# A decoder layer in split fp32: the second cross query goes ahead of the memory product, one root for all query norms, GpSimd adds the cross heads

## What is computed

```python
h = rms_norm(x, attn_norm)
q, k, v, xq = split(h @ w_in, [1024, 1024, 1024, 256])
mix = stick_breaking(q, k, v)                       # 16 heads of 64
mk, mv = split(rms_norm(mem, mem_norm) @ w_mem_kv, [256, 256])
p = softmax(rms_norm(xq, xq_g) @ rms_norm(mk, xk_g).T * SCALE)   # 4 heads, 1024 x 256 each
x = x + concat(mix, p @ mv) @ w_out
x = x + swiglu(rms_norm(x, ffn_norm), w_gate, w_up, w_down)
```

## Time and profile before

| | us |
|---|---|
| median of 3 runs | 1426.36 (1424.12 to 1427.22) |
| the profiled execution | 1431.33, span 1429.5 |
| PE busy | 1377.2 (96% of the span) |
| DVE, ACT, POOL busy | 949.7, 655.3, 186.3 |

### The profile page before, as it was taken

The page is one execution under the profiler, slowest core; times in us unless marked ns, Lnnn a source line. Parts: engine busy times, 40 slices in busy tenths (PEclk is TensorE's granted clock), DMA queues, the critical chain, the costliest instruction groups (busy, mean ns, idle before and its releaser), DMA issues.

```text
span 1429.5 us, 20494 instructions
## 1 busy us (share of the span) xinstructions
PE 1377.2 (96%) x6988; PEld 1127.6 (79%) x6988; DVE 949.7 (66%) x1346; ACT 655.3 (46%) x1120; POOL 186.3 (13%) x155
## 2 busy tenths in 40 slices
PE   6999999899989999699999999999999999999999
PEld 5777788788878888577887788888888888888887
DVE  5567879687968888786347857455565645656455
ACT  7566566566666666573245413324232232422321
POOL 0000000000000000214014311112111120211200
PEclk9989999999999999899999999999999999999999
DMA  6100101001000101003300212111112111121103
GB/s 236 30 17 22 30 23 31 24 23 30 23 23 23 37 17 44 30 23 110 104 16 15 89 52 66 45 47 43 63 42 64 51 44 59 44 60 58 44 30 133
DMA packets 90136, 70.23 MB, mean 49 GB/s; under 512 B 3792, under 2 KB 75472, under 8 KB 90064
## 3 DMA queue, kind: packets, MB, share of 16 engines
q1 hardware_dynamic: 90064, 69.23, 15.6%
HBM read 65.03 MB, written 4.19 MB: 48 GB/s over the span
## 4 chain that ended last, share of the span: by engine, by line
PE 90%; ACT 4%; DVE 2%; issue 2%; POOL 1%; DMA 1%; SPq 0%; ACTq 0%; DVEq 0%; POOLq 0%
PE ps L1284 27%; PE ps L313 17%; PE ps L1380 17%; PE ps L987 7%; PE ps L367 5%; PE ps L351 5%; PE ps L341 4%; PE ps L284 3%; PE ps L1064 1%; ACT junk L687 1%; PE ps L776 1%; POOL f L1144 1%; PE ps L716 1%; PE ps L915 1%; PE ps L877 1%
## 5 line engine op out<-in xcount | busy, mean ns | idle before, releaser
L1390 DVE TENSOR_TENSOR x<-ps,x 128x512 f32<-128x512 f32 x176 | 121.6, 691 | 71.2 <-PE ps L1380 67.0
L436 ACT ACTIVATE a_h<-ps 128x256 fp32r<-128x256 f32 (+2 forms) x96 | 78.0, 812 | 145.6 <-PE ps L351 145.6
L1296 ACT ACTIVATE kept<-ps 128x512 f32<-128x512 f32 x60 | 35.7, 595 | 236.0 <-PE ps L1284 236.0
L313 PE MATMUL ps<-hh,w_h 128*128 128x512 f32 x336 | 142.0, 423 | 0.0
L1380 PE MATMUL ps<-dw_h,gu_l 128*128 128x512 f32 x352 | 138.5, 394 | 0.0
L1380 PE MATMUL ps<-dw_l,gu_h 128*128 128x512 f32 x352 | 137.5, 391 | 0.0
L1380 PE MATMUL ps<-dw_h,gu_h 128*128 128x512 f32 x352 | 137.0, 389 | 0.3 <-issue 0.3
L313 PE MATMUL ps<-hh,w_l 128*128 128x512 f32 x336 | 133.5, 397 | 0.0
L313 PE MATMUL ps<-hl,w_h 128*128 128x512 f32 x336 | 133.1, 396 | 0.0
L545 DVE TENSOR_TENSOR a_l<-ps,a_h 128x256 fp32r<-128x256 f32 (+2 forms) x96 | 91.5, 953 | 60.5 <-ACT a_h L436 59.9
L1284 PE MATMUL ps<-ft_h,part_l 128*128 128x512 f32 x320 | 126.5, 395 | 0.0
(11 more groups left out here) (217 smaller groups left out, 3141.9 us busy)
## 6 DMA issues: line engine op xcount, KB each, us to landing
w_raw<-in_sb_w_in SPq DMA_DIRECT2D x52, 256.0 KB, 2.9
dw_x<-in_w_down SPq DMA_DIRECT2D x22, 512.0 KB, 3.3
part_x<-in_w_gate SPq DMA_DIRECT2D x40, 256.0 KB, 3.5
part_x<-in_w_up SPq DMA_DIRECT2D x40, 256.0 KB, 2.9
wo_raw<-in_w_out SPq DMA_DIRECT2D x20, 256.0 KB, 2.8
x_in<-in_x SPq DMA_DIRECT2D x8, 512.0 KB, 7.8
x<-in_x SPq DMA_DIRECT2D x16, 256.0 KB, 5.7
out<-x SPq DMA_DIRECT2D x16, 256.0 KB, 2.0
```

Of the source, the lines that this page charges most:

```text
L313: mm = pe.matmul(j_ps[:, 0], w[:, kc // 4, kc % 4], h[:, kc, half * BANK:(half + 1) * BANK], start=(kc == 0 and i == 0), stop=(kc == KC - ...
L436: act.activation(a_h[:, :, 0:w // P, col * P:(col + 1) * P], t_ps[:, :, 0:w].rearrange("p h (j q) -> p h j q", q=P), ACT.Copy).then_inc(s_ ...
L1390: dve.tensor_tensor(o, ps[:, (2, 3, 0, 1)[d % 4]], o, ALU.add).then_inc(s_x2, 1)
```

## The change

Stage 2 turns round: right behind the first query's 16 chunks TensorE now projects the second query (number `Q1`), with the memory's transposes between its pieces; its weights have buffers of their own (`wx_h`, `wx_l`). Then comes the memory product, and the sums of squares of both queries stand one by one between its matmuls, with one root for all. The projection of head pair 0 begins ahead of the first scores, 8 half pieces instead of 2. In the cross loop ScalarE copies four row blocks instead of two, and GpSimd adds them instead of VectorE. ScalarE runs one Sqrt ahead of the first x tile and one Sigmoid at step 13, on data that is there, and the warm-up has 5 matmuls of 512 columns that begin behind the fill of `fail`, instead of 12 of 128.

```diff
-    M0 = 2
-    MW = M0 + KC
-    W0 = MW + 2
+    Q1 = 2
+    M0 = 4
+    W0 = M0 + KC
...
-        m_hl = at("m_hl", [P, KC, M], F32R, qk_at + 6 * ROW)
+        m_hl = at("m_hl", [P, KC, M], F32R, x_at + 2 * ROW)
+        wx_h = at("wx_h", [P, 2, 4, P], F32R, ex_at)
+        wx_l = at("wx_l", [P, 2, 4, P], F32R, ex_at + ROW)
...
-        X_FIRST = 2
-        X_COUNT = (1, 2, 1, 2, 0, 2, 1, 2, 1, 2, 0, 2, 1, 2, 2, 1)
-        X_CONV = {0: 2, 2: 3, 6: 4, 8: 5, 13: 6, 15: 7}
-        X_EVAC = {4: 0, 10: 1}
+        X_FIRST = 8
+        X_COUNT = (0, 1, 1, 2, 1, 1, 1, 1, 0, 1, 1, 1, 1, 2, 2, 0)
+        X_CONV = {1: 3, 4: 4, 6: 5, 11: 6, 15: 7}
+        X_EVAC = {0: 0, 8: 1}
...
-        WARM = 12
+        WARM = 5
...
         def pe_mem(pe, k):
+            pe.wait_ge(s_xl, 2 * KC + k // 2 + 1)
             pe.wait_ge(s_wl, M0 + k + 1)
...
-            mm.then_inc(s_pj, 1)
+                    if i == 2 and m == MT - 1:
+                        mm.then_inc(s_pj, 1)
+                    if k >= 4 and i < 2:
+                        pe_cross_stat(pe, 4 * (k - 4) + 2 * i + m)
...
+        def pe_cross_stat(pe, c):
+
+            x_, t = c // NT, c % NT
+            if c == 0:
+                pe.wait_ge(s_id, MADE)
+                pe.wait_ge(s_sq, 2 * XP)
+            mm = pe.matmul(t_ps[:, 1, 2 * c:2 * c + 2], xq_sq[:, x_, t * P:(t + 1) * P], half_ones[:, :],
+                           start=True, stop=True)
...
         def act_cross_low_rows(act, y):
             act.wait_ge(s_cv, y + 1)
             if y:
-                act.wait_ge(s_co, 2 * y)
-            act.activation(pv_low[0:HD, :], o_ps[HD:P, 0:2 * P], ACT.Copy).then_inc(s_cl, 1)
-            act.activation(pv_low[HD:P, :], o_ps[0:HD, 2 * P:4 * P], ACT.Copy).then_inc(s_cl, 1)
...
+                act.wait_ge(s_co, y)
             for h in range(2):
...
+                act.activation(pv_low[r, :], o_ps[other, cols], ACT.Copy).then_inc(s_cl, 1)
+                act.activation(cross_heads_at(y, r), o_ps[r, cols], ACT.Copy).then_inc(s_cl, 1)
+
+        def pool_cross_heads(pool, y):
+            pool.wait_ge(s_cl, 4 * y + 4)
+            heads = cross_heads_at(y, slice(0, P))
+            pool.tensor_tensor(heads, heads, pv_low[:, :], ALU.add).then_inc(s_co, 1)
...
             act.wait_ge(s_id, 1)
+            act.activation(rms[:, 0:1], eps_col[:, :], ACT.Sqrt)
...
-                if 10 <= c < 14:
-                    act_mem_w(act, c - 10)
...
+                if c == 10:
+                    for k in range(2):
+                        act_w_high(act, Q1 + k, 1, k, 0)
...
+                if c == CU - 3:
+                    act.activation(x_stat[:, 0, 0:1], eps_col[:, :], ACT.Sigmoid)
...
             for _ in range(WARM):
-                pe.matmul(ps[:, 3, 0:P], ident[:, :], ident[:, :], start=True, stop=True)
+                pe.matmul(ps[:, 3], ident[:, :], fail[:, 0, 0, 0:BANK], start=True, stop=True)
...
-            for g in range(2 * KC + LEAD, 2 * KC + 4):
-                turn(g)
+            for piece in range(4):
+                pe_project_in(pe, Q1, piece, xq_ps[1])
+                if piece % 2 == 0:
+                    turn(2 * KC + piece)
+                    turn(2 * KC + piece + 1)
             for k in range(KC):
-                pe.wait_ge(s_xl, 2 * KC + k // 2 + 1)
                 pe_mem(pe, k)
...
+            for k in range(4):
+                pe_piece(pe, 0, k // 2, first=True, only=k % 2)
             pe.wait_ge(s_mk, 3 + MT * 2 * XP)
...
-            pe_project_in(pe, MW, 2, xq_ps[1])
+            pe_piece(pe, 0, 2, first=True, only=0)
             pe.wait_ge(s_xl, XU0)
```

More of the change, by code:

```diff
@@ L245, in load_half @@
         def load_half(sp, n, column, k):
-            if not (isinstance(n, int) and n < M0):
-                sp.wait_ge(s_wl, n - MW + 1 if isinstance(n, int) and n < W0 else n - 1)
+            if isinstance(n, int) and W0 <= n < W0 + 2:
+                sp.wait_ge(s_wl, n - W0 + Q1 + 1)
+            elif not (isinstance(n, int) and n < Q1):
+                sp.wait_ge(s_wl, n - 1)
             sp.dma_start(w_raw[:, k % 2], wd[:, 4 * (k % 2):4 * (k % 2) + 4, bass.ds(column, P)]
@@ L400, in act_w_high @@
             act.wait_ge(s_w[k % 2], 16 * (loads + 1))
-            if not (isinstance(n, int) and n < W0):
+            if isinstance(n, int) and W0 <= n < W0 + 2:
+                act.wait_ge(s_pj, Q1)
+            elif not (isinstance(n, int) and n < W0):
                 act.wait_ge(s_pj, n - k % 2 - 2)
-            act.activation(w_h[buf][:, k % 2], w_raw[:, k % 2], ACT.Copy).then_inc(s_wh, 1)
+            act.activation((wx_h if isinstance(n, int) and n // 2 == Q1 // 2 else w_h[buf])[:, k % 2], w_raw[:, k % 2], ACT.Copy).then_inc(s_wh, 1)
         def act_evac_half(act, s, p, par):
@@ L494, in dve_w_low @@
             dve.wait_ge(s_wh, n + 1)
-            dve.tensor_tensor(w_l[buf][:, k % 2], w_raw[:, k % 2], w_h[buf][:, k % 2].bitcast(F32), ALU.subtract
+            high, low = (wx_h, wx_l) if isinstance(n, int) and n // 2 == Q1 // 2 else (w_h[buf], w_l[buf])
+            dve.tensor_tensor(low[:, k % 2], w_raw[:, k % 2], high[:, k % 2].bitcast(F32), ALU.subtract
                               ).then_inc(s_wl, 1)
@@ L937, in pe_cross_values @@
             if y:
-                pe.wait_ge(s_co, 2 * y)
-            else:
-                pe.wait_ge(s_qr, XP)
+                pe.wait_ge(s_cl, 4 * y)
             for h in range(2):
@@ L1510, in _ @@
                 sp.dma_start(mw_raw[:, 2 * k:2 * k + 2], mwd[:, 2 * k:2 * k + 2]).then_inc(s_mw[k], 16)
-            for k in range(2):
-                load_half(sp, MW + k, 3 * D + P, k)
             for k in range(6):
@@ L1569, in _ @@
                                fill=1.0, base=0, pattern=[[-1, P]], channel_multiplier=1).then_inc(s_id, 1)
+            for y in range(CU // 2):
+                pool_cross_heads(pool, y)
             with pool.Fori(0, LOOPS) as m:
@@ L1862, in _ @@
             for j in range(2 * KC):
-                if not KC - LEAD <= j < KC:
+                if not KC - LEAD <= j % KC:
                     turn(j + LEAD)
@@ L1885, in _ @@
             mm.then_inc(s_xt, 1)
-            pe_project_in(pe, MW, 2, xq_ps[1])
+            pe_piece(pe, 0, 2, first=True, only=0)
             pe.wait_ge(s_xl, XU0)
+            pe.wait_ge(s_mv, MT)
+            pe.wait_ge(s_qr, 1)
             pe_cross_scores(pe, 0)
-            pe_project_in(pe, MW, 3, xq_ps[1])
+            pe_piece(pe, 0, 2, first=True, only=1)
             pe_cross_scores(pe, 1)
-            for k in range(X_FIRST):
+            for k in range(6, X_FIRST):
                 pe_piece(pe, 0, k // 2, first=True, only=k % 2)
```

123 lines of the change are left out of this document (57 added, 66 removed).

## The result

| | us |
|---|---|
| before, median of 5 runs | 1426.62 (1424.12 to 1429.02) |
| after, median of 5 runs | 1417.34 (1416.66 to 1418.50) |
| ratio | 0.9935, 95% interval 0.9920 to 0.9949 |
| profiled execution of after | 1417.34, span 1415.6 |

What follows compares the result with a forecast made beforehand. TensorE, busy 96% of the span, was taken as the bound; A, B, C and D summed to 138.4 against 143.14 us, 4.7 less, 4.5 after clock risk: 1421.9 us from the median 1426.36, range 1416.3 to 1426.6.

Steps and rivals of the forecast that it cites:

- A: Head to the end of the first query's 16 chunks: 38.1 us forecast, 40.32 before.
- The 0.9 for the table loads: Head: early table loads on ScalarE save 0.9 us, at most 1.0 because x tile 3 lands at 9.9.
- the 0.4 for the clock: Head: the later, longer warm-up may let the first 16 transposes run faster, 0.4 us saved (0 to 1).
- B: Memory product, second query, first scores, with new content: 42.0 us forecast, 31.15 before.
- rival (2): Sums between the memory's matmuls don't keep the clock; falls there and in step 0 return 3.4 us: 1425.3, chance 0.09.
- 3.8 + 0.8: Memory product: the 16 sums cost 3.8 us, plus 0.8 added for standing between large matmuls.
- C: Cross loop: 50.3 us forecast, 64.26 before.
- The waits around the evacuations: Cross loop: TensorE waits around the projection copies of steps 0 and 8, 2.9 and 2.1 us.
- The clock fall in step 0: Start of the cross loop, thin in TensorE's work: one fall costing 1.7 us, at one in eight counted as 0.2.
- Rival (1): ScalarE becomes the pace of the cross loop, costing 3.5 us: 1425.4, chance 0.16.
- D: End of the cross loop to the pair loop's first projection: 8.0 us forecast, 7.41 before.
- rival (3): Pair loop's jump back: moved code adds a stall per round, 12 us, 1434, chance 0.07; mirror image 1414, 0.03.

Runs made afterwards that it cites:

- the experiment: Kernel after without ScalarE's early square root ahead of the first x tile: 1418.78 us.
- the second profile of after: Kernel after, unchanged, run again on the same chip as other follow-up runs: 1417.69 us.
- the odd steps: Kernel after with the conversions of projection weights 4 and 5 in cross steps 3 and 5 in place of 4 and 6: 1416.24 us.
- the evacuation first: The odd steps, and besides the finished projection copied ahead of the turned weights in cross steps 0 and 8: 1415.26 us.
- WARM 1: Kernel before with 1 warm-up product in place of 12, its pair loop at the same instructions as in the kernel after: 1418.68 us.
- WARM 1, 5, 24 and 32: Kernel before with that many warm-up products in place of 12: 1418.68, 1427.59, 1432.22 and 1417.84 us.
- 7 more products: Kernel after with 7 small identity products put ahead of its 5 warm-up products: 1427.41 us.

## Why the prediction was right in its range and wrong in its reasons

- **A** was right: 37.7 for 38.1. The 0.9 for the table loads was about right (0.75 in the profile, 0.8 by the experiment), but the cap was the landing of x tile 1 at 7.38, behind which ScalarE's next squares follow without a wait, and not that of x tile 3; the 0.4 for the clock was 1.5 here, but not in each execution: in the second profile of after the 16 transposes took 3.63 us again.
- **B** was right: 41.1 for 42.0, no wait ahead of the memory's fifth step, and the interleaved sums keep the clock, so rival (2) is refuted. They cost 14.5 - 10.9 = 3.6 us, not 3.8 + 0.8, and as a block they took 3.63.
- **C** failed, by 4.4 us. The step at fault is "ScalarE has in two steps 5.0 us plus 0.6 where a weight is converted, and TensorE 5.9: it just fits". The sum of ScalarE's work was right (41.1 us in 16 steps, 5.1 in two); what did not fit was the order: the low part of the weight held VectorE's maxima behind ScalarE's last item of the step. From the start of the matmul ahead of a wait to that of the one behind it, less the usual distance, the two waits cost 2.8 us, where nothing was reckoned; the odd steps took 2.3 of it away. Three more terms were off. The waits around the evacuations cost 2.1 and 1.7 us by the same measure, where 2.9 and 2.1 were reckoned. The clock fall in step 0, weighed at 0.2, came and cost 1.0. And what is left, 47.0 us of TensorE's work, was reckoned at 45.3: a half piece takes 1.50 us up to the scores behind it (88.20 to 89.70) and not 1.4, which over 16 of them would be 1.6 (an estimate). 47.0 + 3.8 + 2.8 + 1.0 = 54.6, and the same 47.0 is left in the runs with the odd steps and with the evacuation first. Rival (1) had the time for C about right, its 3.5 more, and the wrong mechanism: with ScalarE as busy the loop took 50.0. That 50.0 is near the forecast's 50.3 is chance, since there less of waits and more of work cancel.
- **D** was right: 7.8 for 8.0, though a wait of 1.26 for GpSimd's last addition was in it that the step didn't name, and the clock behind it (1.4 us) was in no term.
- **The base.** The 4.5 us of half clock and the wait in C were taken from the profiled execution and subtracted from the median. Other profiles lose less there. The cross loop took 64.3 us in the profiled kernel before, at a clock of 0.92, and 63.1 with WARM 1, at 0.97, where the clock was still 1.00 from 72 to 78 us, behind the second block of sums. The kernel before with WARM 1, 5, 24 and 32 has its first mark at 146.1, 148.6, 148.1 and 147.5, the profiled one at 148.9; the kernel after has it at 145.7 and 146.7, with 7 more products 146.1. The means are 147.8 and 146.2. All of the change but the position is worth 1.7 us by them, by the medians with equal stalls 1.0 (1418.68 and 1417.69), 0.2 (1417.84 and 1417.69, or 1427.59 and 1427.41). Forecast were 4.5. In the profile of WARM 1 the pair loop's projection even begins at 140.3, ahead of the two of the kernel after (141.4 and 142.4).
- **The jump back.** "The stalls at the jumps back as before" was wrong, and it is the largest term: 10.0 us in the profiles, 9.4 by the medians of before and WARM 1. Both signs stood in rival (3), at 0.07 and 0.03. The mechanism was named rightly there; "a shift that small rarely crosses a boundary" was reckoned without where the loop lies. Counted in the compiled program, the end at 3063 was 28 to 43 instructions behind a border, and the shift was 44.

So it is luck that the total lies inside the range: a miss of 3 to 4 us in the prologue and a gain of 9 to 10 outside it had opposite signs.

## What to carry to other kernels

A hardware loop whose code takes up most of TensorE's instruction memory (here 1634 of the 2048 instructions that the section of the Trainium skill named above gives it) has a position that decides about a stall at each jump. Count the compiled instructions ahead of it, look whether the instruction queue moves more than the program's size, and before crediting an edit ahead of such a loop, run it with padding that puts the loop back.

In a step where two engines split an operand, let the second engine's half stand where the first engine's half is early in its own queue: add up orders, not only busy times. A term for a clock that fell in the profiled execution is to be taken from more than one: here two places of some 1 to 3 us fell in some profiles and not in others, with the same instructions and waits ahead of them.

## What the runs showed of the hardware

The stall at the jump is not one number: 3.8 to 6.7 us a jump over the kernels with eight blocks.

GpSimd's addition with two operands in SBUF runs beside VectorE. In the kernel after, VectorE's product for the bias took 0.46 us beside it and 0.16 otherwise, and two scalings took 1.03 for 0.62:

```profile
90.85 0.73 POOL L977 TENSOR_TENSOR o_t<-o_t,pv_low 128x256 f32<-128x256 f32 x1 [86.31 <-ACT o_t L972]
91.15 0.46 DVE L903 TENSOR_TENSOR x_stat<-x_stat,q_stat 128x2 f32<-128x2 f32 x1
95.09 0.16 DVE L903 TENSOR_TENSOR x_stat<-x_stat,q_stat 128x2 f32<-128x2 f32 x1
...
114.31 0.73 POOL L977 TENSOR_TENSOR o_t<-o_t,pv_low 128x256 f32<-128x256 f32 x1 [7.77 <-ACT o_t L972]
114.43 1.03 DVE L922 TENSOR_SCALAR succ<-succ,x_stat 128x256 f32<-128x256 f32 x2
117.07 0.62 DVE L922 TENSOR_SCALAR succ<-succ,x_stat 128x256 f32<-128x256 f32 x2
```

The second profile of the kernel after has the same (0.46 and 1.03), and with the heads by VectorE, where GpSimd adds nothing in the loop, every such product takes 0.16 and every pair of scalings 0.61 or 0.62. VectorE's low part of `a`, which reads one input from PSUM, keeps its 0.69 beside an addition (127.70) as alone (134.26). The addition at 127.12 took 0.85 for 0.73, having begun while VectorE was scaling. The rule of the Trainium skill named with rival (1), that GpSimd's way to SBUF is shared with VectorE, with contention for VectorE's instructions with two inputs there, agrees with the product for the bias, which has two. The scaling has one besides its factor, and `w_l`, which has two, kept its 0.69 beside the last 0.12 us of an addition (98.89), so which operations contend isn't settled here. Over the loop VectorE lost about 1.0 us by it (0.30, 0.33 and 0.42), and no wait of TensorE in the profile is traced to that, so it isn't the outcome of rival (1).
